# The last scatter of a streaming MoE step: identity products that add x in PSUM, multiplies that read PSUM, sample stores on ScalarE, and a 1 MB transfer in two rows

## Chip, core and metric

The kernel runs on one core of one Trainium2 chip. The metric is device time in microseconds. Engines are named as in the profile: PE is TensorE (PEld its weight loads), DVE is VectorE, ACT is ScalarE, POOL is GpSimd, SP is SyncE; a q behind a name is the engine's own instruction queue, which also issues DMAs.

## The reference

One layer of an encoder trunk for 256 prompt tokens and 32 sample tokens of width 1024, all in float32: a modulated RMS norm, an input projection, a pooling mixer and a convolution module, gates and an output projection, and then a mixture of experts and a final norm. The change touches only what follows the last expert:

```python
x = x + g1 * (merged @ w_out)
h2 = _rms_norm(x, norm2_g) * (1.0 + sc2) + sh2
# 32 experts of 1024 x 1024, top 4 by a router:
#   gt = min(t @ Wg + bg, 7);  up = clip(t @ Wu + bu, -7, 7)
#   out += combine[:, e] * ((gt * sigmoid(1.702 gt) * (up + 1)) @ Wd + bd)
x = x + g2 * _moe(h2, ...)
y = x * rsqrt(mean(x * x) + 1e-6) * final_g        # prompt and sample
```

## The kernel before

Tokens lie on partitions: `x[:, 0]` and `x[:, 1]` hold 128 prompt tokens each, and the 32 sample tokens are spread as `xs`, four quarters of 256 features on four groups of 32 partitions.

The experts run as items, an item being up to 64 tokens of one expert; here there are 33 for 32 experts. In an item PE multiplies the gathered tokens by the expert's gate, up and down matrices (`product`, whose inner matmul is L1731: 16 matmuls of 512 columns for one matrix, each of which has two rows in the trace). DVE evaluates the down product into `ysb`, scaled by the gate g2 (L1306). PE then puts the item's rows back at their tokens by products with the weighted one-hot matrix `ohwT` (L1758 for the prompt, L1749 for the sample). It does so inside the next item, and DVE adds the result to `x` (L1269, L1265). A product of the scatter has only 64 rows to sum over: half hh of the features lies on partitions 64 hh to 64 hh + 63, so two products, one for each half, use different halves of the PE array and different PSUM banks.

The last item has no next one, so its scatter stands alone behind the loop. PE waits for `y_ev` (the first half of `ysb`, all of it for the sample) and makes the products for prompt tile 0, the sample and tile 1 (L1845, L1749). DVE adds each to `x` (`last_add`, L1316; the sample at L1336), ACT squares the sums and accumulates them (`last_squares`, L851; L856), DVE takes the mean (`last_mean`, L1319), ACT the root (`last_root`, L846), and DVE the reciprocal and the product with `final_g` (`finish`, L1328, L1330). The sample's sum of squares has four parts on four groups of partitions; a product on PE adds these up (L1849). SP stores the outputs in the order in which they are made: tile 0 (L539), the sample in four pieces (L537), tile 1 in two halves (L544).

Weights stream from HBM on SP's queue through 18 slots of SBUF, a pair of slots (2 MB) at a time. PE raises `piece_used` when a piece may be overwritten, and SP waits for it before each load. `LAST_HALVES` names the pairs of the last expert that come in two transfers of 1 MB each, so that `product` can start on the first half (L513). The very last is the second half of the last down pair; PE waits for it before k = 6, the seventh of the eight steps over the contraction. The order of all instructions is written out by hand, for each engine.

## Time and profile before

| | us |
|---|---|
| time, median of 3 runs (lowest, highest) | 1152.16 (1151.28, 1153.07) |
| profiled execution: span from first to last instruction | 1150.3 |
| PE busy | 1122.8 (98%) |
| DVE busy | 497.9 (43%) |
| ACT busy | 181.4 (16%) |
| HBM read | 454.40 MB, 396 GB/s over the span |
| span behind the last expert product (1137.7 to 1150.3) | 12.6 |

The trace gives the span of the profiled execution; the time of a run holds what lies around such a span too. The median of the timed runs is 1.86 us above the span. Busy time says how long an engine had an instruction in work; matmul rows overlap, since one starts before the last results of the one before have come out.

### The profile page before, as it was taken

The numbers are of one execution on the slowest core, as the hardware profiler recorded it, in microseconds if no ns is written. First come the engines' busy times: TensorE is split into PE (matmuls) and PEld (weight loads), VectorE is DVE, ScalarE is ACT, GpSimd is POOL, SyncE is SP. The second block draws the span as 40 slices with busy tenths as digits, with TensorE's granted clock in tenths as the row PEclk, the third lists the DMA queues.
The fourth block names the chain that finished last, engine by engine and source line by source line (L and its number), as shares of the span: only waits on it lengthen the run. The fifth ranks groups of instructions, "written<-read, shape, count | busy, mean of one in ns | idle before, by whom it ended". The sixth has DMA issues, their size and how long they took to land.

```text
span 1150.3 us, 16135 instructions
## 1 busy us (share of the span) xinstructions
PE 1122.8 (98%) x5962; PEld 457.5 (40%) x5963; DVE 497.9 (43%) x1134; ACT 181.4 (16%) x343; POOL 29.8 (3%) x78
## 2 busy tenths in 40 slices
PE   8999999999999999999999999999999999999996
PEld 6676675633333333333333333333333333333332
DVE  3498425653344433444333433343334433333334
ACT  4101301311111111111111111111111111111112
POOL 4002300000000000000000000000000000000000
PEclk9999999999999999999999999999999999999999
DMA  9988688699999999999999999999999999999995
GB/s 342 374 288 297 245 305 303 229 419 417 427 428 428 428 428 428 428 428 428 428 428 428 428 428 428 428 428 428 428 428 428 428 428 428 428 428 429 426 422 228
DMA packets 59022, 456.15 MB, mean 397 GB/s; under 512 B 7237, under 2 KB 26497, under 8 KB 31349
## 3 DMA queue, kind: packets, MB, share of 16 engines
q1 hardware_dynamic: 54880, 452.35, 94.9%
q10 hardware_dynamic: 4117, 3.47, 1.2%
q8 instruction: 16, 0.26, 0.1%
q14 instruction: 9, 0.07, 0.0%
HBM read 454.40 MB, written 1.40 MB: 396 GB/s over the span
## 4 chain that ended last, share of the span: by engine, by line
PE 77%; DMA 21%; DVE 1%; issue 0%; SPq 0%; ACT 0%; DVEq 0%
PE bank L1731 46%; DMA arena<-in_exp_w_up 10%; DMA arena<-in_exp_w_gate 10%; PE bank L1509 6%; PE bank L1456 4%; PE bank L1758 4%; PE bank L1675 4%; PE bank L1596 2%; PE bank L1813 1%; PE bank L1579 1%; PE bank L1683 1%; PE bank L1430 1%; PE bank L1749 1%; PE bank L1687 1%; PE bank L1378 1%; PE bank L1689 0%
## 5 line engine op out<-in xcount | busy, mean ns | idle before, releaser
L1731 PE MATMUL bank<-ring,arena 128*64 128x512 f32 x2112 | 469.9, 595 | 10.2 <-DMA ring<-in_exp_w_gate 9.7
L1731 PEld LDWEIGHTS bank<-ring,arena 128*64 128x64 f32 x2112 | 146.3, 137 | 310.0 <-issue 283.7
L1731 PE MATMUL bank<-arena 128*64 128x512 f32 x1056 | 235.9, 595 | 4.2 <-DMA arena<-in_exp_w_gate 4.0
L1731 PEld LDWEIGHTS bank<-arena 128*64 128x64 f32 x1056 | 73.6, 137 | 153.8 <-issue 138.5
L821 ACT ACTIVATE arena<-arena 32x256 f32<-32x256 f32 x136 | 56.0, 412 | 421.1 <-DVE arena L1200 419.9
L1291 DVE TENSOR_SCALAR arena<-bank 128x512 f32<-128x512 f32 x33 | 22.8, 691 | 166.6 <-PE bank L1731 166.6
L1284 DVE TENSOR_SCALAR arena<-bank 128x512 f32<-128x512 f32 x33 | 22.8, 691 | 166.5 <-PE bank L1731 166.5
L1306 DVE TENSOR_TENSOR arena<-bank,biases 128x512 f32<-128x512 f32 x66 | 42.5, 686 | 109.9 <-PE bank L1731 109.9
L1269 DVE TENSOR_TENSOR x<-x,bank 128x512 f32<-128x512 f32 x132 | 84.5, 681 | 12.6 <-PE bank L1758 12.6
L834 ACT ACTIVATE arena<-arena 128x512 f32<-128x512 f32 x33 | 20.8, 629 | 353.8 <-DVE arena L1284 353.8
L1758 PE MATMUL bank<-arena 64*128 64x512 f32 x264 | 65.6, 615 | 0.0
L1509 PE MATMUL bank<-arena,ring 128*128 128x288 f32 x256 | 64.4, 409 | 0.0
L1675 PE MATMUL bank<-h,arena 128*64 128x512 f32 x268 | 63.3, 592 | 0.0
L969 DVE SCALAR_TENSOR_TENSOR h<-h,arena 128x318 f32<-128x318 f32 x120 | 55.5, 541 | 0.0
L1509 PEld LDWEIGHTS bank<-arena,ring 128*128 128x128 f32 x256 | 48.1, 190 | 17.1 <-issue 4.2
L1456 PE MATMUL bank<-arena,ring 128*128 128x288 f32 x192 | 47.7, 408 | 0.5 <-DVE arena L922 0.5
L834 ACT ACT_TABLE_LOAD x33 | 42.3, 1283 | 0.6
L1456 PEld LDWEIGHTS bank<-arena,ring 128*128 128x128 f32 x192 | 36.2, 190 | 12.0 <-issue 1.7
L1687 PE MATMUL bank<-biases,mine 32*64 32x288 f32 x264 | 40.0, 414 | 0.0
L1758 PEld LDWEIGHTS bank<-arena 64*128 64x128 f32 x264 | 22.7, 186 | 42.3 <-issue 42.3
L1205 DVE COPY arena<-arena 32x256 f32<-32x256 f32 x136 | 38.4, 282 | 2.5
L1683 PE MATMUL bank<-biases,mine 32*64 32x512 f32 x136 | 37.4, 613 | 0.0
(312 smaller groups left out, 739.8 us busy)
## 6 DMA issues: line engine op xcount, KB each, us to landing
ring<-in_exp_w_gate SPq DMA_DIRECT2D x42, 2048.0 KB, 27.8
ring<-in_exp_w_up SPq DMA_DIRECT2D x41, 2048.0 KB, 28.2
ring<-in_exp_w_down SPq DMA_DIRECT2D x40, 2048.0 KB, 29.1
arena<-in_exp_w_gate SPq DMA_DIRECT2D x21, 2048.0 KB, 25.7
arena<-in_exp_w_up SPq DMA_DIRECT2D x20, 2048.0 KB, 27.3
arena<-in_exp_w_down SPq DMA_DIRECT2D x20, 2048.0 KB, 30.0
ring<-in_w_ada SPq DMA_DIRECT2D x24, 1024.0 KB, 10.7
ring<-in_gate_w SPq DMA_DIRECT2D x8, 1024.0 KB, 8.6
```

The source lines that it names most:

```text
L821: ins = a.activation(*square_moves(1, s, u), ACT.Copy)
L834: a.activation(gsig, gmin, ACT.Sigmoid, scale=ALPHA).then_inc(gsig_ready, 1)
L969: ins = v.scalar_tensor_tensor(out=yc[:, c, :], in0=uc_ext[:, c, k:k + CW], scalar=tap, in1=yc[:, c, :], op0=ALU.mult, op1=ALU.add)
L1269: ins = v.tensor_tensor(x[:, t, cs], x[:, t, cs], scatter_bank(t, hh), ALU.add)
L1306: v.tensor_tensor(ysb[:, gg, :], bank[5][:, :], g2h[:, gg, :], ALU.mult).then_inc(y_ev, 1)
L1456: ins = mm(bank[n % 4][:, 0:TOK], w[:, k, P * (n % 2):P * (n % 2 + 1)], (hS if n < UNSHIFTED else hT)[:, k, :], start=(k == 0), stop=(n >= ...
L1509: ins = mm(bank[n % 4][:, 0:TOK], w[:, k, P * (n % 2):P * (n % 2 + 1)], hT[:, k, :], start=(k == 0), stop=(k == KD - 1))
L1675: ins = mm(bank[0][64 * hh:64 * hh + 64, :], oh[:, t, :], half_rows(h2[:, t, :], hh), start=start, stop=stop, skip_group_check=True)
L1683: mm(bank[3][out, :], mine[B_GATE, :], bias_rows[B_GATE, cs], start=True, stop=False, skip_group_check=True)
L1687: found = mm(bank[6 + i][out, 0:TOK], mine[LOOKUP, :], routedT[:, i, :], start=True, stop=True, skip_group_check=True)
L1731: ins = mm(out[64 * hh:64 * hh + 64, :], lhs(k), w[:, D * (k % 2) + HALF * hh:D * (k % 2) + HALF * (hh + 1)], start=(done is y_mm and k == ...
L1758: ins = mm(scatter_bank(t, hh), ohwT[64 * hh:64 * hh + 64, P * t:P * (t + 1)], ysb[64 * hh:64 * hh + 64, 0, :], start=True, stop=True, ski ...
```

## The change

It does five things, four of them behind the last item.

- Identity products add `x` in PSUM. `carry` multiplies the identity by `x`, which starts the sum in the bank, and the scatter product adds to it there. Tile 0's two banks and the sample's are filled ahead of the wait for `y_ev`; tile 1's two banks are filled one by one between scatter products. The sample's sum is in bank 1 in place of bank 5.
- The four additions on DVE for the prompt and the one for the sample are gone. ACT squares what is in PSUM, DVE's final multiplies read PSUM, and tile 0 is multiplied in two halves rather than in one instruction.
- The mean of a tile is no longer an addition and a scaling on DVE: DVE scales the first half's sum, and ACT's root takes the second half's sum as input with the first as its bias. The two memsets of accumulators move ahead of the item loop.
- ACT issues the sample's four stores, behind its last root. SP issues tile 0 and tile 1's halves.
- The last transfer of 1 MB, 128 partitions of 8 KB, becomes two of 4 KB per partition. PE waits for the first before k = 6 and for the second (`last_ld`) before k = 7.

```diff
-            def refill_halves(e, q, before):
+            def refill_halves(e, q, before, rows_apart=False):
 ...
+                    if half and rows_apart:
+                        for r, landed in enumerate((pair_ld[p], last_ld)):
+                            at_row = SLOT * half + D * r
+                            sp.dma_start(slots(2 * p + half, 1)[:, D * r:D * (r + 1)], w[:, i % 2, at_row:at_row + D]).then_inc(landed, 16)
+                        continue
 ...
+                refill_halves(last_turn, at_last + i, (at_last + i - PAIRS) // PER_EXPERT, rows_apart=(i == LAST_HALVES[-1]))
 ...
-            for i, t in enumerate((0, 2, 1)):
-                sp.wait_ge(y_ready, i + 1)
-                if t == 2:
-                    for q in range(4):
-                        sp.dma_start(quarter(y_sample[0], q), y_s[32 * q:32 * q + 32, :]).then_inc(stored, 16)
-                elif t == 0:
-                    sp.dma_start(y_prompt[0, 0:P, :], ybuf[:, 0, :]).then_inc(stored, 16)
-                else:
-                    for hh in range(2):
-                        sp.wait_ge(y_ready, i + 1 + hh)
-                        cs = slice(HALF * hh, HALF * (hh + 1))
-                        sp.dma_start(y_prompt[0, P:2 * P, cs], ybuf[:, 1, cs]).then_inc(stored, 16)
+            sp.wait_ge(y_ready, 2)
+            sp.dma_start(y_prompt[0, 0:P, :], ybuf[:, 0, :]).then_inc(stored, 16)
+            for hh in range(2):
+                sp.wait_ge(y_ready, 4 + hh)
+                cs = slice(HALF * hh, HALF * (hh + 1))
+                sp.dma_start(y_prompt[0, P:2 * P, cs], ybuf[:, 1, cs]).then_inc(stored, 16)
 ...
-            def last_root(t, nth):
+            def last_root(t, nth, scale=1.0, rest=None):
                 act.wait_ge(mean2, 3 + nth)
-                a.activation(stat[:, 4 + t:5 + t], stat[:, 8 + t:9 + t], ACT.Sqrt).then_inc(sqrt_ready, 1)
-
-            def last_squares(t):
-                for hh in range(2):
-                    act.wait_ge(x3_ready, 3 * t + hh + 1)
-                    a.activation(ring[:, JUNK + t, HALF * hh:HALF * (hh + 1)], x[:, t, HALF * hh:HALF * (hh + 1)],
-                                 ACT.Square, accum_out=stat[:, 18 + 3 * hh + t:19 + 3 * hh + t]).then_inc(ssq3, 1)
-
-            last_squares(0)
-            act.wait_ge(x3_ready, 3)
-            a.activation(ring[:, JUNK + 2, 0:D // 4], xs, ACT.Square, accum_out=part_sum[:, 0:1]).then_inc(parts_ready, 1)
-            last_root(0, 1)
-            last_squares(1)
+                a.activation(stat[:, 4 + t:5 + t], rest if rest is not None else stat[:, 8 + t:9 + t], ACT.Sqrt, scale=scale,
+                             bias=stat[:, 8 + t:9 + t] if rest is not None else 0.0).then_inc(sqrt_ready, 1)
+
+            def last_squares(t, hh):
+                act.wait_ge(last_mm, 3 * t + hh + 1)
+                a.activation(ring[:, JUNK + t, HALF * hh:HALF * (hh + 1)], last_bank(t, hh),
+                             ACT.Square, accum_out=stat[:, 18 + 3 * hh + t:19 + 3 * hh + t]).then_inc(ssq3, 1)
+
+            last_squares(0, 0)
+            last_squares(0, 1)
+            act.wait_ge(last_mm, 3)
+            a.activation(ring[:, JUNK + 2, 0:D // 4], last_sample, ACT.Square, accum_out=part_sum[:, 0:1]).then_inc(parts_ready, 1)
+            act.wait_ge(ssq3, 2)
+            last_root(0, 1, 1.0 / D, stat[:, 21:22])
+            last_squares(1, 0)
+            last_squares(1, 1)
             last_root(2, 2)
-            last_root(1, 3)
+            act.wait_ge(ssq3, 4)
+            last_root(1, 3, 1.0 / D, stat[:, 22:23])
+            act.wait_ge(y_ready, 3)
+            for q in range(4):
+                act.dma_start(quarter(y_sample[0], q), y_s[32 * q:32 * q + 32, :]).then_inc(stored, 16)
 ...
+            v.memset(part_sum, 0.0)
+            v.memset(stat[:, 18:24], 0.0)
 ...
-            dve.wait_ge(ssq2, 6)
             dve.wait_ge(y_ev, items * 2 + 2)
             dve.sem_inc(last_y, 1)
-            v.memset(part_sum[:, :], 0.0)
-            v.memset(stat[:, 18:24], 0.0)
-            def last_add(t, hh):
-                cs = slice(HALF * hh, HALF * (hh + 1))
-                dve.wait_ge(last_mm, 3 * t + hh + 1)
-                v.tensor_tensor(x[:, t, cs], x[:, t, cs], last_bank(t, hh), ALU.add).then_inc(x3_ready, 1)
 
             def last_mean(t, total):
                 v.tensor_scalar(stat[:, 8 + t:9 + t], total, 1.0 / D, EPS, ALU.mult, ALU.add).then_inc(mean2, 1)
 
-            def tile_mean(t):
-                dve.wait_ge(ssq3, 2 * t + 2)
-                step(v.tensor_tensor(stat[:, t:t + 1], stat[:, 18 + t:19 + t], stat[:, 21 + t:22 + t], ALU.add))
-                last_mean(t, stat[:, t:t + 1])
-
-            def finish(t, nth, parts):
+            def last_gain(t, nth):
                 dve.wait_ge(sqrt_ready, 4 + nth)
                 step(v.reciprocal(stat[:, 4 + t:5 + t], stat[:, 4 + t:5 + t]))
-                for out, src, gain in parts:
-                    v.scalar_tensor_tensor(out=out, in0=src, scalar=stat[:, 4 + t:5 + t], in1=gain,
-                                           op0=ALU.mult, op1=ALU.mult).then_inc(y_ready, 1)
-
-            last_add(0, 0)
-            last_add(0, 1)
-            dve.wait_ge(last_mm, 3)
-            v.tensor_tensor(xs, xs, bank[5][:, 0:D // 4], ALU.add).then_inc(x3_ready, 1)
-            last_add(1, 0)
-            tile_mean(0)
-            last_add(1, 1)
+
+            def finish(t, out, src, gain):
+                v.scalar_tensor_tensor(out=out, in0=src, scalar=stat[:, 4 + t:5 + t], in1=gain,
+                                       op0=ALU.mult, op1=ALU.mult).then_inc(y_ready, 1)
+
+            halves = [slice(HALF * hh, HALF * (hh + 1)) for hh in range(2)]
+            dve.wait_ge(ssq3, 1)
+            last_mean(0, stat[:, 18:19])
+            dve.wait_ge(fg_ld, 16 * 5)
+            last_gain(0, 1)
+            finish(0, ybuf[:, 0, halves[0]], last_bank(0, 0), fgb[:, halves[0]])
             dve.wait_ge(parts_mm, 1)
             last_mean(2, bank[2][:, 0:1])
-            dve.wait_ge(fg_ld, 16 * 5)
-            finish(0, 1, [(ybuf[:, 0, :], x[:, 0, :], fgb)])
-            tile_mean(1)
-            finish(2, 2, [(y_s, xs, fgq)])
-            halves = [slice(HALF * hh, HALF * (hh + 1)) for hh in range(2)]
-            finish(1, 3, [(ybuf[:, 1, cs], x[:, 1, cs], fgb[:, cs]) for cs in halves])
+            dve.wait_ge(ssq3, 3)
+            last_mean(1, stat[:, 19:20])
+            finish(0, ybuf[:, 0, halves[1]], last_bank(0, 1), fgb[:, halves[1]])
+            last_gain(2, 2)
+            finish(2, y_s, last_sample, fgq)
+            last_gain(1, 3)
+            for hh, cs in enumerate(halves):
+                finish(1, ybuf[:, 1, cs], last_bank(1, hh), fgb[:, cs])
 ...
+                    elif last and done is y_mm and k == KD - 1:
+                        pe.wait_ge(last_ld, 16)
 ...
-            def scatter_sample():
+            def scatter_sample(out=bank[5][:, 0:D // 4], start=True):
 
                 for half in range(2):
                     for hh in range(2):
                         q = 2 * hh + half
-                        ins = mm(bank[5][32 * q:32 * q + 32, 0:D // 4], ohwT[64 * hh:64 * hh + 64, 2 * P:TOK],
-                                 ysb[64 * hh:64 * hh + 64, 1, D // 4 * half:D // 4 * (half + 1)], start=True, stop=True,
+                        ins = mm(out[32 * q:32 * q + 32, :], ohwT[64 * hh:64 * hh + 64, 2 * P:TOK],
+                                 ysb[64 * hh:64 * hh + 64, 1, D // 4 * half:D // 4 * (half + 1)], start=start, stop=True,
                                  skip_group_check=True)
 ...
-            pe.wait_ge(y_ev, items * 2 + 1)
             pe.wait_ge(ohwT_ev, items + 1)
             pe.wait_ge(scat_add, items * 2 + 1)
             pe.wait_ge(up_read, items + 1)
-            for t in (0, 2, 1):
-                if t == 2:
-                    pe.wait_ge(last_y, 1)
-                    scatter_sample().then_inc(last_mm, 1)
-                    continue
-                for hh in range(2):
-                    mm(last_bank(t, hh), ohwT[64 * hh:64 * hh + 64, P * t:P * (t + 1)], ysb[64 * hh:64 * hh + 64, 0, :],
-                       start=True, stop=True, skip_group_check=True).then_inc(last_mm, 1)
+
+            def carry(out, src):
+                mm(out, ident[:, :], src, start=True, stop=False, skip_group_check=True)
+
+            def last_scatter(t, hh):
+                mm(last_bank(t, hh), ohwT[64 * hh:64 * hh + 64, P * t:P * (t + 1)], ysb[64 * hh:64 * hh + 64, 0, :],
+                   start=False, stop=True, skip_group_check=True).then_inc(last_mm, 1)
+
+            for hh in range(2):
+                carry(last_bank(0, hh), x[:, 0, HALF * hh:HALF * (hh + 1)])
+            carry(last_sample, xs)
+            pe.wait_ge(y_ev, items * 2 + 1)
+            for hh in range(2):
+                last_scatter(0, hh)
+            carry(last_bank(1, 0), x[:, 1, 0:HALF])
+            pe.wait_ge(last_y, 1)
+            scatter_sample(last_sample, start=False).then_inc(last_mm, 1)
+            last_scatter(1, 0)
+            carry(last_bank(1, 1), x[:, 1, HALF:D])
+            last_scatter(1, 1)
```

PE behind the last expert product. L1845 are the scatter products of a prompt tile, L1749 (L1751 after) those of the sample, L1842 the identity products, and the last row the sum of the sample's parts. Before:

```order
L1845 MATMUL bank6<-arena 128x512 [waits up_read,scat_add,ohwT_ev]
L1845 MATMUL bank7<-arena 128x512
L1749 MATMUL bank5<-arena 32x256 [waits last_y]
L1749 MATMUL bank5<-arena 32x256 x3
L1845 MATMUL bank3<-arena 128x512
L1845 MATMUL bank4<-arena 128x512
L1849 MATMUL bank2<-arena 128x4 [waits parts_ready,same_made]
```

After:

```order
L1842 MATMUL bank6<-x,ident 128x512 [waits up_read,scat_add]
L1842 MATMUL bank7<-x,ident 128x512
L1842 MATMUL bank1<-arena,ident 128x256
L1845 MATMUL bank6<-arena 128x512 [waits y_ev]
L1845 MATMUL bank7<-arena 128x512
L1842 MATMUL bank3<-x,ident 128x512
L1751 MATMUL bank1<-arena 32x256 [waits last_y]
L1751 MATMUL bank1<-arena 32x256 x3
L1845 MATMUL bank3<-arena 128x512
L1842 MATMUL bank4<-x,ident 128x512
L1845 MATMUL bank4<-arena 128x512
L1862 MATMUL bank2<-arena 128x4 [waits parts_ready,same_made]
```

Three identity products now stand ahead of the scatter of tile 0 (banks 6 and 7), and one stands ahead of each scatter product of tile 1 (banks 3 and 4), so that these two no longer follow each other. The wait for `y_ev` has moved behind the first three.

DVE at the same place, from the first addition to the first final multiply (L1330, 1024 columns) and the mean behind it. L1319 is `last_mean`; L1323 adds two halves' sums. Before:

```order
L1316 TENSOR_TENSOR x<-x,bank6 128x512 [waits last_mm]
L1316 TENSOR_TENSOR x<-x,bank7 128x512 [waits last_mm]
L1336 TENSOR_TENSOR arena<-arena,bank5 128x256 [waits last_mm]
L1316 TENSOR_TENSOR x<-x,bank3 128x512 [waits last_mm]
L1323 TENSOR_TENSOR stat<-stat 128x1 [waits ssq3]
L1319 TENSOR_SCALAR stat<-stat 128x1 [waits chain_v]
L1316 TENSOR_TENSOR x<-x,bank4 128x512 [waits last_mm]
L1319 TENSOR_SCALAR stat<-bank2 128x1 [waits parts_mm]
L1328 RECIPROCAL stat<-stat 128x1 [waits sqrt_ready,fg_ld]
L1330 SCALAR_TENSOR_TENSOR h2<-x,stat,ring 128x1024 [waits chain_v]
L1323 TENSOR_TENSOR stat<-stat 128x1 [waits ssq3]
L1319 TENSOR_SCALAR stat<-stat 128x1 [waits chain_v]
```

After, from the first mean (L1322) to the last final multiply (L1329):

```order
L1322 TENSOR_SCALAR stat<-stat 128x1 [waits y_ev,ssq3]
L1326 RECIPROCAL stat<-stat 128x1 [waits sqrt_ready,fg_ld]
L1329 SCALAR_TENSOR_TENSOR h2<-bank6,stat,ring 128x512 [waits chain_v]
L1322 TENSOR_SCALAR stat<-bank2 128x1 [waits parts_mm]
L1322 TENSOR_SCALAR stat<-stat 128x1 [waits ssq3]
L1329 SCALAR_TENSOR_TENSOR h2<-bank7,stat,ring 128x512
L1326 RECIPROCAL stat<-stat 128x1 [waits sqrt_ready]
L1329 SCALAR_TENSOR_TENSOR h2<-bank1,stat,ring 128x256 [waits chain_v]
L1326 RECIPROCAL stat<-stat 128x1 [waits sqrt_ready]
L1329 SCALAR_TENSOR_TENSOR h2<-bank3,stat,ring 128x512 [waits chain_v]
L1329 SCALAR_TENSOR_TENSOR h2<-bank4,stat,ring 128x512
```

The additions are gone, and so are the ones of sums. The wait for `parts_mm`, the last product on PE, stood ahead of all final multiplies; now it stands behind the first of them and ahead of the other four.

## Rows read from the trace of the kernel before

**Rows 1.** Busy time by stage: us, then each engine's busy us, clock, DMA, GB/s
```profile
1110.35:1137.70 27.35, 27.34 (x144) 9.46 (x144) 10.21 (x23) 4.17 (x8) 0.00 (x0) 1.00 0.90 368
1137.70:1150.30 12.60, 3.11 (x18) 1.08 (x18) 8.20 (x21) 3.46 (x13) 0.00 (x0) 0.83 0.26 94
```

**Rows 2.** TensorE's last expert product, timeline: start us, us, engine, line
```profile
1130.61 7.09 PE L1731 MATMUL bank<-ring,arena 128*64 128x512 f32 x32
```

**Rows 3.** TensorE's weight loads around the last transfer's landing, timeline
```profile
1135.42 0.14 PEld L1731 LDWEIGHTS bank<-ring,arena 128*64 128x64 f32 x2 [0.32 <-DMA ring<-in_exp_w_down]
1135.81 0.14 PEld L1731 LDWEIGHTS bank<-ring,arena 128*64 128x64 f32 x2 [0.25 <-issue]
```

**Rows 4.** SyncE's DMA issues: last weight transfers and the three kinds of store
```profile
1098.01 10.93 SPq L513 DMA_DIRECT2D ring<-in_exp_w_down  x2
...
1144.49 0.37 SPq L539 DMA_DIRECT2D out<-h  x1
1145.34 1.73 SPq L537 DMA_DIRECT2D out<-h  x4
1147.17 0.84 SPq L544 DMA_DIRECT2D out<-h  x2
```

**Rows 5.** All engines from the last expert product's end, timeline
```profile
1137.75 1.29 DVE L1306 TENSOR_TENSOR arena<-bank,biases 128x512 f32<-128x512 f32 x2 [3.33 <-PE bank L1731]
...
1138.68 1.13 PE L1845 MATMUL bank<-arena 64*128 64x512 f32 x4 [0.98 <-DVE arena L1306]
...
1139.74 0.64 PE L1749 MATMUL bank<-arena 64*32 64x256 f32 x8
...
1139.81 1.28 DVE L1316 TENSOR_TENSOR x<-x,bank 128x512 f32<-128x512 f32 x2 [0.49 <-PE bank L1845]
...
1140.31 1.13 PE L1845 MATMUL bank<-arena 64*128 64x512 f32 x4
...
1140.53 0.63 ACT L851 ACTIVATE ring<-x 128x512 f32<-128x512 f32 x1 [5.27 <-DVE x L1316]
...
1142.41 0.36 PE L1849 MATMUL bank<-arena 128*128 128x4 f32 x2 [0.98 <-ACT ring L856]
...
1142.92 0.15 DVE L1319 TENSOR_SCALAR stat<-bank 128x1 f32<-128x1 f32 x1
...
1143.17 0.61 ACT L851 ACTIVATE ring<-x 128x512 f32<-128x512 f32 x1
...
1143.78 0.19 ACT L846 ACTIVATE stat<-stat 128x1 f32<-128x1 f32 x1
...
1144.83 0.48 DVE L1330 SCALAR_TENSOR_TENSOR h<-arena,stat,ring 128x256 f32<-128x256 f32 x1
...
1145.42 1.41 DVE L1330 SCALAR_TENSOR_TENSOR h<-x,stat,ring 128x512 f32<-128x512 f32 x2
```

**Rows 6.** TensorE where one expert follows another with no stall, timeline
```profile
302.82 7.09 PE L1731 MATMUL bank<-arena 128*64 128x512 f32 x32
309.74 1.46 PE L1731 MATMUL bank<-ring,arena 128*64 128x512 f32 x6
```

**Rows 7.** TensorE: products over 128 rows, then scatter products over 64 rows
```profile
184.90 7.13 PE L1596 MATMUL bank<-ring,arena 128*128 128x512 f32 x16
...
1117.37 1.99 PE L1758 MATMUL bank<-arena 64*128 64x512 f32 x8
```

**Rows 8.** A ScalarE read of PSUM, by line and form: busy us, mean ns
```profile
L673 ACT ACTIVATE arena<-bank 128x512 f32<-128x512 f32 x1 | 0.6, 597 | 0.6 <-PE bank L1378 0.6
```

**Rows 9.** What SyncE waited for at the end, and ScalarE's slowest DMA issues
```profile
SPq L90 <- DMA out<-h: 1.9, 1, 1.9
...
L732 ACTq DMA_DIRECT2D out<-biases x16: 875/885/1015, 133.6 to 150.9; - x16
```

**Rows 10.** Landing times of 1 MB and 512 KB transfers, first 230 us, by tile
```profile
ring<-in_exp_w_down SPq DMA_DIRECT2D x2, 1024.0 KB, 5.4
...
ring<-in_pool_w SPq DMA_DIRECT2D x1, 512.0 KB, 3.7
```

4 lines of the change are left out of this document (2 added, 2 removed).

## The prediction

> **What bounds the kernel now.** I read first the busy time by stage. From 1110.35 us PE is busy for 27.34 of 27.35 us, so the last expert runs at PE's pace. Behind it lie 12.6 us in which PE is busy for 3.11, DVE for 8.20 and ACT for 3.46 [rows 1]: a chain of short steps, each waiting for the one before. All but one edit of the change lie in these 12.6 us, and that one, the split transfer, ends just ahead of them.
>
> Then the timeline of that chain [rows 5]. The last expert product starts at 1130.61 [rows 2], and DVE takes up its result at 1137.75. PE starts the scatter at 1138.68 and has it done 1.13 later for tile 0 and at 1141.44 for tile 1. DVE adds from 1139.81, ACT squares from 1140.53 to 1143.78, and DVE's multiplies end at 1146.83 (1145.42 + 1.41).
>
> Last, SP's queue [rows 4]. Tile 0 is stored at 1144.49. The sample's four issues take 1145.34 to 1147.07. Tile 1's first half is ready at about 1146.13 (half of the 1.41), but is issued at 1147.17, and the second half, ready at 1146.83, at about 1147.59. So the queue of stores, and not DVE, sets the last 0.75 us. SP then waits 1.9 for the data [rows 9].
>
> **The change, part by part.**
>
> Transfer in two rows. The last product's 16 matmuls take 0.43 each (6.92 / 16 [rows 6]), a step k has two of them, so k = 6 starts 12 x 0.43 behind 1130.61, at 1135.8, and its weights are loaded one matmul ahead. That load was released by the DMA at 1135.42 and the next stands at 1135.81 [rows 3]: the megabyte came some 0.04 late at most, and the product still took the 7.09 us of one that waits for nothing [rows 2, 6]. I cost the gain at 0. In a run where the megabyte is later, the split can take away one step k, 0.86, at most. SP issued the megabyte some 25 us ahead (1098.01 + 10.93 [rows 4]), so one more issue costs it nothing. The loss is a rival below.
>
> Identity products on PE. Eight products over 128 rows of 512 columns took 7.13 us [rows 7]. In a stream a row outlasts the next one's start by 0.17 (7.09 against 6.92 [rows 6]), so one costs (7.13 - 0.17) / 8 = 0.87, and the one of 256 columns 0.44. The same rows show also that PE passes from one expert to the next, registers and branch included, with no gap, so the first three start at 1130.61 + 6.92 = 1137.53 and end at 1139.71. They hide the wait for `y_ev`, which let PE start at 1138.68 [rows 5], but are longer than it by 1.03. Tile 0's pair of scatter products then takes 1.13 to its end [rows 5], 1140.84. ACT squares from there, and no longer from 1140.53: the addition of about 0.7 that is gone is more than eaten.
>
> Tile 1 is worse off. Two pairs of scatter products took 1.99 [rows 7], some 0.95 for a pair, that is, two products over 64 rows ran in little more than the time of one full product. The change parts tile 1's pair. No row shows such a product alone. From below it is half a pair, 0.48; from above a whole pair, 0.95; I take the 0.87 of a full product, because the columns to stream are the same and a pair costs hardly more. Then: identity from 1140.66, sample 1141.53, and 0.57 later (1139.74 to 1140.31 [rows 5]) the scatter at 1142.10, identity 1142.97, scatter 1143.84. PE is free at 1144.71, where before tile 1 was done by 1141.44: 3.3 later.
>
> ACT and DVE behind it. ACT's last square starts at about 1144.9 and its roots follow 0.61 later [rows 5], done by 1145.8. DVE's chain is longer. The sum of the sample's parts starts at 1144.71, and DVE reads it 0.51 later (1142.41 to 1142.92 [rows 5]), at 1145.22. Until then the second multiply of tile 0 is queued behind that wait, with DVE idle from about 1143.8. Then come two means, 0.25 (0.15 each by the row, partly overlapped, an estimate); tile 0's second half, 0.69 (half of 1.28 or 1.41 [rows 5]); a reciprocal, 0.11; the sample and its reciprocal, 0.59 (1144.83 to 1145.42 [rows 5]); and tile 1's halves, 1.41. The last output is ready at 1148.27, against 1146.83 before: 1.44 later.
>
> ACT reading PSUM instead of SBUF: 0.597 for a copy of 512 columns [rows 8] against 0.61 to 0.63 for the squares [rows 5]: nothing. DVE reading PSUM: additions from PSUM took 0.64 each, multiplies from SBUF 0.70 [rows 5]: nothing to pay either. The Trainium skill, VectorE: DVE Perf Modes, in its errata section, gives VectorE a fixed part of 58 cycles for SBUF sources and 120 for PSUM, at 0.96 GHz: 0.065 us more for each read of PSUM, an estimate from that page. By it the four multiplies that end the chain would cost 0.26 more and the sum would be 1153.0. The rows do not bear it out.
>
> The memsets ahead of the loop are two of DVE's shortest instructions, and PE has the whole first gate product to cover them: 0.
>
> Stores. SP has tile 0 at 1146.2, tile 1's first half at 1147.57 and its second at 1148.3; before these were issued at 1144.49, 1147.17 and 1147.59. The last issue is 0.7 later, the last but one 0.4. When the second half is issued, the first is still on its way, so the end follows something between: I take 0.55. Moving the sample's issues to ACT thus gives back 0.75 us or so of the 1.44 lost. On ACT they start at 1146.9 and, at SP's 0.43 each [rows 4], are done at 1148.6, level with SP's.
>
> Sum: identity products and unpaired scatter +1.44, the queue of stores -0.75 to -1.05, the rest 0: +0.4 to +0.7, say +0.55. The profiled execution would have a span of 1150.85 in place of 1150.3. The timed median lies 1.86 above the span, so 1152.16 + 0.55 = 1152.7 us. What this measurement can tell from no change is 0.2%, 2.3 us, and the forecast is a quarter of that.
>
> **Rivals.**
>
> Better overlap. If an unpaired product costs 0.48, PE is free 0.78 earlier and all behind it too: 1151.9. If in the timed runs the last megabyte is later than in the trace, the split takes up to 0.86 away: 1151.1. Against it: the product with no stall in the trace. For a gain of over 2.3 us I find no row: all that is removed on the chain is five additions and the queue of stores.
>
> Stores on ACT. This one ends slower. ACT's own issues of small stores took 0.875 to 1.015 each [rows 9], where SP's took 0.43. With four at 1.015 from 1146.9 the last is issued at 1150.96, the data take up to 1.9, and the close 0.4 as before: span 1153.3, which is 3.0 more, 1155.2. It decides from about 0.83 each. Against it: those had many short pieces of 512 bytes, and the sample's have 32 of 1 KB.
>
> The second row late. Alone, a 1 MB transfer of expert weights landed in 5.4 and one of 512 KB in 3.7 [rows 10]. Two of 3.7 one behind the other would be 2.0 longer: the last row at 1137.4 rather than 1135.4, needed for the load of k = 7 at 1136.3, so PE stops for 1.1: 1153.8. Against it: both rows are issued long before their turn in a queue that is full, so they follow each other without a gap. The rule that 1 MB is the size from which the bandwidth is near its best (the Trainium skill, DMA: Bandwidth & Descriptors, section Bandwidth) would speak for this rival, and a fixed part of 2.0 us for each transfer, which the same page gives, would cost about as much. Only the landing in the changed trace can tell.
>
> That the change doesn't do what it says is no rival I can give a time: that SP's sample stores go and the additions go stands in the order.
>
> **How the numbers follow.** Forecast 0.68 (1152.7, own range 1151.9 to 1153.6); better overlap 0.17 (1151.1 to 1151.9); stores on ACT 0.08 (1153.6 to 1155.2); second row late 0.07 (1153.8). The runs before spread by 0.9 to either side of the median, which I add to the ends. For 8 in 10, I leave out the far ends of the rivals: 1151.2 to 1154.4. Faster by over 2.3 us needs something that I do not see, 0.04; slower by as much (above 1154.5) is the upper half of the ACT rival, and the others with the runs' spread of 0.9 on top, 0.09; within it 0.87.
>
> **What would show it.** In the changed trace: three identity products from 1137.5, counted from a last expert product at the same place; tile 0's scatter a microsecond later than before; tile 1's last scatter ending 3 us later; DVE idle ahead of the mean of the sample; the last multiply ending 1.4 later, and tile 1's stores issued as soon as it is ready. Wrong would be: a gap in the last down product before k = 7, ACT's issues outlasting SP's, unpaired products at half the time, or any shift ahead of 1110 us, since nothing there should move.

## The result, and the profile after

The changed kernel took 1156.63 us (median of 6 runs, 1155.12 to 1162.28), the kernel before 1151.91 beside it (6 runs, 1151.28 to 1153.07): ratio 1.0040, 95% interval 1.0023 to 1.0058. Measured again with 12 and 36 runs it was 1.0019 [1.0010, 1.0029], +2.2 us (1.2 to 3.3). So it is slower, by 1.2 us at the least and some 2 by the second, tighter measurement, where +0.55 (1152.7) was forecast. The profiled execution took 1155.12, its span is 1153.4, against 1150.3 before: 3.1 more.

All that the change touches, but the split transfer and the two early memsets, lies behind the last expert product. I cut the span in two ways: at that product's end for the busy times, and at its start for the lengths that are compared below. Busy time by stage (stretch, length, then PE, PEld, DVE, ACT and POOL, granted clock, DMA share, GB/s); the first two rows answer to [rows 1], the third is the part of the second in which PE is never idle:

```profile
1111.16:1138.51 27.35, 27.35 (x145) 9.54 (x145) 10.29 (x23) 4.17 (x8) 0.00 (x0) 1.00 0.91 374
1138.51:1153.40 14.89, 8.50 (x28) 2.92 (x28) 5.27 (x13) 3.66 (x13) 0.00 (x0) 0.83 0.22 80
1138.51:1147.01 8.50, 8.50 (x28) 2.92 (x28) 2.36 (x5) 2.93 (x10) 0.00 (x0) 1.00 0.00 1
```

The last stage is 14.89 long instead of 12.6. PE is busy for 8.50 of it instead of 3.11, DVE for 5.27 instead of 8.20: the work went from an engine that had time in the gaps to one that now runs 8.50 us without one, at a clock of 1.00. The other part of the 3.1 lies ahead: the last product starts 0.81 later than in [rows 2]. From its start to the end of the span ("the tail", below) it is 1153.4 - 1131.42 = 21.98 us, before 1150.3 - 1130.61 = 19.69: **+2.29**. Spans are given to 0.1 us, so a tail is good to 0.05 and the difference of two tails to 0.1.

TensorE in the tail, timeline of the changed kernel (start us, busy us; the rows of the weight loads, PEld, say in brackets how long the loader had been idle):

```profile
1131.42 7.09 PE L1733 MATMUL bank<-ring,arena 128*64 128x512 f32 x32
...
1138.43 1.98 PE L1842 MATMUL bank<-x,ident 128*128 128x512 f32 x4
...
1140.26 0.59 PE L1842 MATMUL bank<-arena,ident 128*128 128x256 f32 x2
...
1140.78 1.13 PE L1845 MATMUL bank<-arena 64*128 64x512 f32 x4
1141.84 0.30 PEld L1842 LDWEIGHTS bank<-x,ident 128*128 128x128 f32 x2 [0.76 <-issue]
1141.84 1.12 PE L1842 MATMUL bank<-x,ident 128*128 128x512 f32 x2
...
1142.90 0.64 PE L1751 MATMUL bank<-arena 64*32 64x256 f32 x8
...
1143.46 1.12 PE L1845 MATMUL bank<-arena 64*128 64x512 f32 x2
...
1144.51 1.13 PE L1842 MATMUL bank<-x,ident 128*128 128x512 f32 x2
...
1145.57 1.12 PE L1845 MATMUL bank<-arena 64*128 64x512 f32 x2
1146.62 0.30 PEld L1862 LDWEIGHTS bank<-arena 128*128 128x128 f32 x2 [0.76 <-issue]
1146.62 0.39 PE L1862 MATMUL bank<-arena 128*128 128x4 f32 x2
```

The product of 32 matmuls takes 7.09, as it did with the megabyte whole. Read the starts. A full product in the middle of a stream of its own shape (rows x columns of weights) takes 0.86 from its start to the next: two matmuls of 0.43. The first one behind another shape takes 0.11 more, since its two matmuls start 0.54 apart (1138.43 and 1138.97), and the last one ahead of another shape 0.09 more. So each change of shape costs 0.2. From 1140.78 on, every product stands between two other shapes, and the next start comes 1.05 to 1.06 later: 1141.84, then 1142.90, then 1143.46 to 1144.51, 1145.57, 1146.62. The loader's rows show what is different. At such a place the next weights are loaded only when the next product starts (1141.84 and 1141.84), not ahead of it. From tile 0's pair to the sum of parts there are six changes of shape; with 0.86 for a product or a pair and 0.2 for a change that is 5 x 0.86 + 0.36 for the sample (0.56 - 0.2) + 6 x 0.2 = 5.86, where the rows have 1146.62 - 1140.78 = 5.84. From the first identity product to the sum of parts it is 8.19 us; the prediction had 7.18.

DVE and ACT behind it:

```profile
1141.94 0.60 ACT L852 ACTIVATE ring<-bank 128x512 f32<-128x512 f32 x1 [5.87 <-PE bank L1845]
...
1144.60 0.75 DVE L1329 SCALAR_TENSOR_TENSOR h<-bank,stat,ring 128x512 f32<-128x512 f32 x1
...
1146.73 0.60 ACT L852 ACTIVATE ring<-bank 128x512 f32<-128x512 f32 x1 [1.42 <-PE bank L1845]
1147.05 0.16 DVE L1322 TENSOR_SCALAR stat<-bank 128x1 f32<-128x1 f32 x1 [1.70 <-PE bank L1862]
...
1147.18 0.74 DVE L1329 SCALAR_TENSOR_TENSOR h<-bank,stat,ring 128x512 f32<-128x512 f32 x1
...
1148.62 1.41 DVE L1329 SCALAR_TENSOR_TENSOR h<-bank,stat,ring 128x512 f32<-128x512 f32 x2
```

DVE waits 1.70 for PE's sum, with the second multiply of tile 0 queued behind that wait, and ends at 1150.03: 18.61 behind the product's start, before 16.22 (1145.42 + 1.41 - 1130.61). Of the +2.29, +2.39 is there by the last multiply. The stores give back 0.10.

The stores: the issues in the timeline, then what SyncE waited for at the end, then one line of ScalarE's issues (min/median/max in ns) and their landing (us):

```profile
1147.95 0.37 SPq L541 DMA_DIRECT2D out<-h  x1
...
1148.55 2.00 ACTq L868 DMA_DIRECT2D out<-h  x4
...
1149.40 0.99 SPq L545 DMA_DIRECT2D out<-h  x2
```

```profile
SPq L90 <- DMA out<-h: 2.6, 1, 2.6
```

```profile
L868 ACTq DMA_DIRECT2D out<-h x4: 353/446/656, 1148.5 to 1150.1; - x4
...
DMA to landing us min/median/max: 2.2/2.4/2.9
```

SP issues tile 1's second half as soon as it is there, and then waits 2.6 where it had waited 1.9 [rows 9]. ACT's four issues fill 2.00 us. The last starts at 1150.1 and the slowest lands in 2.9: 1153.0. The sample's last store, and not tile 1's, is then the last to land.

The 0.81 ahead of the tail is not in the code that the change edits. In the changed kernel's profiled execution TensorE's granted clock stood at 0.50 (the 1.2 GHz level) from 22 to 25 us, with PE busy throughout. In the 8 us ahead PE had been busy for 7.25, as in that of before. The pooled mixing (L1368) starts at 31.46:

```profile
22.00:24.00 2.00, 2.00 (x5) 1.43 (x6) 1.92 (x10) 1.19 (x4) 0.00 (x0) 0.50 1.11 311
```

```profile
31.46 1.05 PE L1368 MATMUL bank<-arena 4*32 4x512 f32 x4
```

In before the clock was 1.00 (2.4 GHz) there and the row stands at 29.83:

```profile
22.00:24.00 2.00, 2.00 (x9) 1.58 (x10) 1.93 (x10) 1.20 (x4) 0.00 (x0) 1.00 1.12 317
```

```profile
29.83 1.05 PE L1368 MATMUL bank<-arena 4*32 4x512 f32 x4
```

1.63 us are lost by there, and 0.81 of them are left at the last product. The difference is found again in PE's idle time ahead of the expert products, 9.4 us in all, 8.9 of it by the transfers (page of after, busy us, mean ns, idle before):

```profile
L1733 PE MATMUL bank<-ring,arena 128*64 128x512 f32 x2112 | 469.9, 595 | 9.4 <-DMA ring<-in_exp_w_gate 8.9
```

The same row of before has 10.2 and 9.7: PE came later to transfers that set the pace there, and waited less.

### The profile page after: what moved, and what is told of

It is laid out like the page before. It is cut to its first block, busy times and chain, and to the rows that moved or that the text cites. A ratio compares the mean times of both kernels' runs of the same rounds, so it can differ in the third digit from the quotient of the medians.

```text
span 1153.4 us, 16151 instructions
## 1 busy us (share of the span) xinstructions
PE 1129.3 (98%) x5972; PEld 460.1 (40%) x5973; DVE 498.1 (43%) x1128; ACT 181.4 (16%) x343; POOL 29.7 (3%) x78
## 4 chain that ended last, share of the span: by engine, by line
PE 78%; DMA 21%; DVE 1%; issue 0%; SPq 0%; ACT 0%; DVEq 0%
PE bank L1733 45%; DMA arena<-in_exp_w_up 10%; DMA arena<-in_exp_w_gate 10%; PE bank L1509 5%; PE bank L1456 4%; PE bank L1760 4%; PE bank L1675 4%; PE bank L1596 2%; PE bank L1815 1%; PE bank L1579 1%; PE bank L1683 1%; PE bank L1430 1%; PE bank L1751 1%; PE bank L1687 1%; PE bank L1378 1%; PE bank L1689 0%
## 5 line engine op out<-in xcount | busy, mean ns | idle before, releaser
L1279 DVE TENSOR_TENSOR x<-x,bank 128x512 f32<-128x512 f32 x132 | 84.6, 682 | 12.6 <-PE bank L1760 12.6
L1689 PE MATMUL bank<-h,arena 32*64 32x512 f32 x136 | 37.4, 613 | 0.0
```

Source lines behind the costliest of these rows:

```text
L1279: ins = v.tensor_tensor(x[:, t, cs], x[:, t, cs], scatter_bank(t, hh), ALU.add)
```

## The experiments

**Theory T:** the tail's 2.3 us come from PE: products of another shape one behind the other cost 1.06 instead of 0.87, so all behind the sum of parts is later, and the stores on ACT add a little at the end. **Rival R1:** the split transfer costs it. **R2:** the stores on ACT cost it. **R3:** VectorE's queue, or its reads of PSUM. The table has what was measured; each run is then told with what was expected. Ratios are those to the kernel before on the same chip, of 11 or 12 runs each (the first of after is of 6), against 17 to 36 of the kernel before; "tail" and "last multiply" come from one profiled execution each and are counted from the start of the last expert product.

| run | ratio [95%] | tail | last multiply ends | SP's last wait |
|---|---|---|---|---|
| before | | 19.69 | 16.22 | 1.9 |
| after | 1.0040 [1.0023, 1.0058] | 21.98 | 18.61 | 2.6 |
| e1 after again | 1.0019 [1.0010, 1.0029] | 22.05 | 18.61 | 2.7 |
| e2 megabyte whole | 1.0021 [1.0010, 1.0031] | 22.03 | 18.61 | 2.6 |
| e3 before + split | 1.0005 [0.9994, 1.0015] | 19.75 | 16.22 | 1.9 |
| e4 before + ACT stores | 0.9996 [0.9986, 1.0006] | 19.32 | 16.22 | 2.3 |
| e5 tile 0 in halves | 1.0010 [0.9993, 1.0028] | 21.61 | 18.61 | 2.2 |
| e6 grouped products | 1.0006 [0.9993, 1.0020] | 20.97 | 17.70 | 2.5 |
| e7 DVE order | 1.0009 [0.9995, 1.0023] | 21.27 | 18.32 | 2.2 |
| e8 after, SP stores | 1.0032 [1.0014, 1.0049] | 22.34 | 18.61 | 1.9 |
| e9 sample's identity only | 0.9997 [0.9980, 1.0014] | 19.29 | 16.26 | 2.2 |
| e10 tile 1 added | 1.0011 [1.0002, 1.0020] | 20.44 | 17.40 | 2.2 |
| e11 no identity | 1.0016 [0.9992, 1.0040] | 19.90 | 16.96 | 2.2 |
| e12 e9, mean earlier | 0.9995 [0.9986, 1.0003] | 18.59 | 15.66 | 2.2 |

**e1: the changed kernel once more**, without an edit.

> The changed kernel once more, for a second trace and a second time. The two traces so far differ by 3.1 us in span, of which 0.8 lies ahead of the last expert. My theory: these 0.8 come from the 3.4 us at the lower clock at 22 to 25 us of that one execution and are no part of the change; then a trace without that dip has the last product start near 1130.6, and the median is the tail's 2.3 us above the kernel before (1154.2). The rival, something ahead of the tail that the change makes slower: the last product starts at 1132 or later although the clock is 1.0 throughout, and the time is again 4 to 5 above the kernel before.

Tail 22.05 and 1.0019, +2.2 us: the tail repeats within 0.07, and this time it is the whole of the difference. The clock is 1.00 at 22 us, and the last product starts at 1130.45, as the theory wanted. The first measurement's +4.7 did not come back: the changed kernel's median was 1.6 lower than there (1155.05) and that of the kernel before 1.2 higher (1153.07).

**e2: the changed kernel, last megabyte in one transfer.**

```
-  refill_halves(last_turn, ..., rows_apart=(i == LAST_HALVES[-1]))
+  refill_halves(last_turn, ...)
-      elif last and done is y_mm and k == KD - 1:
-          pe.wait_ge(last_ld, 16)
```

> The changed kernel with the last megabyte in one transfer again. If the split row by row costs nothing, as I forecast, it has the time of the changed kernel within 0.5 us. If the split is where the time goes that the tail doesn't explain (a later landing, or loads of the last expert that drain more slowly), it is 1.5 to 2.5 faster.

**e3: the kernel before with the split alone** (the second row counted on another semaphore that is free by then).

```
+  if half and rows_apart:
+      for r, landed in enumerate((pair_ld[p], c_ld)):
+          sp.dma_start(... row r ...).then_inc(landed, 16)
 ...
+      elif last and done is y_mm and k == KD - 1:
+          pe.wait_ge(c_ld, 48)
```

> The kernel before with only the last megabyte split. By my theory within 0.5 us of the kernel before; by the rival 1.5 to 2.5 slower. The second row is counted on a semaphore of the first loads, because there is none to spare.

```profile
1130.95 7.09 PE L1738 MATMUL bank<-ring,arena 128*64 128x512 f32 x32
```

Again 7.09, and the tail moves by 0.02 (e2 against e1) and 0.06 (e3 against before). By time e3 is 1.0005, and e2's 1.0021 stands beside e1's 1.0019; its median is 0.65 above e1's, a little outside the 0.5 that I allowed, but the intervals cover each other. R1 falls from both sides: the split neither costs nor gives. In a run whose megabyte came late it might still give; none of the fourteen traces has one.

**e4: the kernel before with the sample's stores on ACT.**

```
 # SP: the four sample stores go
+act.wait_ge(y_ready, 2)
+for q in range(4):
+    act.dma_start(quarter(y_sample[0], q), y_s[32 * q:32 * q + 32, :]).then_inc(stored, 16)
```

> The kernel before with only the sample's four stores issued by ScalarE. By my sum SP can issue tile 1's halves at 1146.2 and 1146.9 in place of 1147.2 and 1147.6, so it is 0.5 to 0.75 faster (1151.3). By the rival, stores from two queues finish each other later (2.6 us of waiting at the end of the changed kernel against 1.9 before), and the gain is 0 to 0.2.

```profile
1145.66 0.37 SPq L538 DMA_DIRECT2D out<-h  x1
...
1146.51 2.07 ACTq L862 DMA_DIRECT2D out<-h  x4
...
1147.41 0.95 SPq L543 DMA_DIRECT2D out<-h  x2
```

The tail is 0.37 shorter, between the 0.5 to 0.75 of my sum and the 0 to 0.2 of the rival: R2 falls, the stores on ACT are a gain, but half of what the queue had cost (0.75). SP's last wait grew from 1.9 to 2.3. This is shown by the tail alone; the times (0.9996) leave it open.

**e5: tile 0 stored in two halves**, so that its first half leaves early.

```
-sp.wait_ge(y_ready, 2)
-sp.dma_start(y_prompt[0, 0:P, :], ybuf[:, 0, :]).then_inc(stored, 16)
+for hh in range(2):
+    sp.wait_ge(y_ready, 1 + hh)
+    sp.dma_start(y_prompt[0, 0:P, cs], ybuf[:, 0, cs]).then_inc(stored, 16)
```

> The changed kernel with tile 0 stored in two halves as soon as each is multiplied. The changed kernel waits 2.6 us for its stores, the one before 1.9. Theory S: 1.19 MB of stores now leave within 2.5 us and the wait is for bandwidth; then 256 KB leave 1.7 us earlier, the wait falls to 2.1 or less, and the tail from the last expert product's start (22.0 us) gets 0.4 to 0.6 shorter. Rival: the wait is longer because stores of two queues (SP and ACT) mix; then the halves change nothing.

Tail 21.61, 0.37 less than after's, all of it behind the last multiply, which still ends 18.61 behind the product. ACT's issues took 1.79 instead of 2.00, and landed in 1.6 to 2.3 instead of 2.2 to 2.9. So the store of the whole of tile 0, issued 0.6 ahead of the sample's, had stood in their way. The gain is just short of the forecast (0.4 to 0.6, with a wait of 2.1 or less: it was 2.2). It is not that store alone: in e8, where it is as close, the sample's stores land in 1.6 to 2.3 as well, but there SP issues them and tile 1's halves wait behind. What slows them in the changed kernel is a store ahead and stores of the other queue beside them; how much each is was not parted further.

**e6: the same products, grouped by shape**: from tile 0's pair to the sum of parts four changes of shape instead of six, and tile 1's pair kept.

```
-carry(last_bank(1, 0), x[:, 1, 0:HALF])
+for hh in range(2):
+    carry(last_bank(1, hh), x[:, 1, HALF * hh:HALF * (hh + 1)])
 scatter_sample(...)
-last_scatter(1, 0)
-carry(last_bank(1, 1), x[:, 1, HALF:D])
-last_scatter(1, 1)
+for hh in range(2):
+    last_scatter(1, hh)
```

> The changed kernel with tile 1's two identity products one behind the other, then the sample, then tile 1's two scatter products as a pair. Theory P: a product costs 0.86 when the next has its shape and 1.06 when it doesn't (the next weights are loaded late), and two scatter products of different halves run together. Then PE is done 1.06 + 0.2 = 1.25 us earlier (the last product starts 6.95 behind the first identity product in place of 8.19), and the tail is 1.0 to 1.3 shorter. Rival: scatter onto a started sum is slow by itself (1.06 each, pair or not); then PE gains 0.2 only.

```profile
1137.85 1.98 PE L1842 MATMUL bank<-x,ident 128*128 128x512 f32 x4
...
1140.19 1.13 PE L1845 MATMUL bank<-arena 64*128 64x512 f32 x4
...
1141.25 1.98 PE L1842 MATMUL bank<-x,ident 128*128 128x512 f32 x4
...
1143.16 0.64 PE L1751 MATMUL bank<-arena 64*32 64x256 f32 x8
1143.73 1.13 PE L1845 MATMUL bank<-arena 64*128 64x512 f32 x4
...
1144.79 0.38 PE L1862 MATMUL bank<-arena 128*128 128x4 f32 x2
```

The same eleven products take 6.94 from the first identity product to the sum, as T had said (6.95), against 8.19. The two identity products of tile 1 take 1.91 (0.96 and 0.95, 0.2 above two of 0.86), and the two scatter products of tile 1 1.06 together, where they had been 1.05 each, so the rival falls. Of the 1.25, two changes fewer are 0.4 and the pair that is kept 0.86. Tail -1.01. That is the test of T: an order of PE's products, with nothing else changed, is worth a microsecond. The time (1.0006) does not stand apart from e1's by its interval; the trace does.

**e7: VectorE's second multiply of tile 0 ahead of its wait for the sum.**

```
 finish(0, ybuf[:, 0, halves[0]], last_bank(0, 0), fgb[:, halves[0]])
+finish(0, ybuf[:, 0, halves[1]], last_bank(0, 1), fgb[:, halves[1]])
 dve.wait_ge(parts_mm, 1)
 ...
-finish(0, ybuf[:, 0, halves[1]], last_bank(0, 1), fgb[:, halves[1]])
```

> The changed kernel with tile 0's second multiply ahead of the wait for the sample's sum of parts, on VectorE. In the changed trace VectorE is idle for 1.70 us there with that multiply behind it. If that order is on the chain, its 0.70 goes off it and tile 0 is stored 1.8 us earlier: the tail is 0.7 to 1.2 shorter. Rival: ScalarE's roots bound what follows; then the tail gains at most 0.2 from the sample on.

```profile
1142.91 1.41 DVE L1329 SCALAR_TENSOR_TENSOR h<-bank,stat,ring 128x512 f32<-128x512 f32 x2
...
1144.35 0.37 SPq L541 DMA_DIRECT2D out<-h  x1
...
1145.36 0.16 DVE L1322 TENSOR_SCALAR stat<-bank 128x1 f32<-128x1 f32 x1 [1.04 <-PE bank L1862]
...
1145.86 0.16 DVE L1326 RECIPROCAL stat<-stat 128x1 f32<-128x1 f32 x1 [0.28 <-ACT stat L847]
```

The last multiply ends only 0.29 earlier although 0.74 of work left the chain, because DVE then waits 0.28 for ACT's roots, which that multiply had covered. ACT's last square is bound by PE too. The tail is 0.71 shorter. The rest lies in the stores: tile 0 is now stored 2.2 us ahead of the sample (1144.35 against 1146.57), and ACT's stores land in 1.5 to 2.4, as in e5. R3's queue is real, but second to PE.

**e8: the changed kernel, sample's stores back on SP.**

```
 # SP, between tile 0 and tile 1
+sp.wait_ge(y_ready, 3)
+for q in range(4):
+    sp.dma_start(quarter(y_sample[0], q), y_s[32 * q:32 * q + 32, :]).then_inc(stored, 16)
 # ACT: the same four go
```

> The changed kernel with the sample's stores issued by SP again, between tile 0's and tile 1's. By the queue's arithmetic: four issues of 0.43 from 1148.5 hold tile 1's first half until 1150.25 and its second until 1150.7, where ACT's issue let them go at 1149.4 and 1150.1, so the tail is 0.6 longer. By the rival of mixed queues: the shorter wait at the end gives most of that back, 0 to 0.2 longer.

```profile
1149.28 1.99 SPq L544 DMA_DIRECT2D out<-h  x4
...
1151.32 0.90 SPq L548 DMA_DIRECT2D out<-h  x2
```

Tail 22.34, 0.36 longer than after's, between the queue's arithmetic and the rival; in e4 the same move was worth 0.37. SP's four issues cost 1.99 here, before 1.73 [rows 4].

**e9: only the sample gets an identity product.** The tiles' scatter products run in pairs, tile 1 ahead of the sample, and VectorE adds them to x as before. Kept from the change: ACT's stores, the sample read from PSUM, the early memsets. Tile 0 is stored in halves, the megabyte is whole.

```
+carry(last_sample, xs)
 pe.wait_ge(y_ev, items * 2 + 1)
+pair(0); pair(1)
 pe.wait_ge(last_y, 1)
+scatter_sample(last_sample, start=False).then_inc(last_mm, 1)
 # DVE: four additions to x, the sample's goes
```

> The kernel before with an identity product for the sample only (0.43, inside PE's wait for y_ev), both prompt tiles' scatter pairs one behind the other and then the sample, additions on VectorE as before, the root that takes the second half's sum, tile 0 stored in halves and the sample stored by ScalarE. Tail means the time from the last expert product's start to the span's end: 19.7 in the kernel before, 22.0 in the changed one. If VectorE's work is what bounds the kernel before there, 0.41 of addition and some 0.3 of small steps go, and with the stores the tail is 18.5 to 19.0. Rival: ScalarE's row of squares bounds it instead (five squares and three roots, 3.5 us, from 1140.5); then it is 19.2 to 19.5.

```profile
1136.62 0.70 PE L1846 MATMUL bank<-arena,ident 128*128 128x256 f32 x2
...
1137.49 1.99 PE L1850 MATMUL bank<-arena 64*128 64x512 f32 x8 [0.16 <-DVE arena L1313]
...
1141.04 0.15 DVE L1326 TENSOR_SCALAR stat<-stat 128x1 f32<-128x1 f32 x1
...
1141.62 0.29 ACT L841 ACTIVATE stat<-stat 128x1 f32<-128x1 f32 x1 [0.56 <-DVE stat L1326]
```

Without the tiles' identity products the tail is 19.29: 2.69 less than after's (0.37 of it by the halves of tile 0), 0.40 less than before's. Against before the gain is one of the stores, as in e4: the last multiply ends at 16.26, before at 16.22. I had expected 18.5 to 19.0, and the rows show why it was missed: VectorE's mean of tile 0 stands behind four additions, and ACT waits 0.56 for it with two squares queued.

**e10: identity products for tile 0 and the sample, tile 1 added by VectorE.**

```
+for hh in range(2):
+    carry(last_bank(0, hh), x[:, 0, HALF * hh:HALF * (hh + 1)])
 carry(last_sample, xs)
 pe.wait_ge(y_ev, items * 2 + 1)
+pair(0, start=False); pair(1)
```

> The kernel e9_sample_identity with identity products for tile 0 as well, which VectorE and ScalarE then read in PSUM; tile 1 still added on VectorE. It asks what tile 1's identity products alone cost in the changed kernel. By the account that PE is the bound there (8.19 us from the first identity product to the sum of parts), PE is now free 3 us sooner and the tail falls from 22.0 to 19.8 to 20.2, still above e9, because the two identity products of tile 0 start the chain 0.9 later and VectorE fills up behind. Rival: products onto started sums are as cheap as others and the changed kernel's loss is in VectorE's order; then it stays above 21.

Tail 20.44, a little more than expected: 1.15 above e9's for tile 0's identity products. They outlast the wait that was to hide them: the scatter starts 9.37 behind the expert product (1139.93 - 1130.56), in e9 7.88 (1137.49 - 1129.61). What is left to after's 21.98 is 1.54, of which the store of tile 0 in halves explains 0.37 (e5): tile 1's identity products and parted pair cost some 1.2.

**e11: no identity product at all**, otherwise e9 (the sample's addition is back on VectorE).

> The kernel e9_sample_identity with no identity product at all: the sample is added on VectorE, between the tiles. If the sample's identity product is worth its addition, the tail is 0.3 to 0.5 longer than that of e9. If it is worth nothing because ScalarE is the bound, the two are equal within 0.1.

Tail 19.90, 0.61 more than e9's, somewhat above the 0.3 to 0.5 of the forecast. The sample's product, which fits into PE's wait for `y_ev` (0.16 of that wait is left in e9, and the scatter starts no later for it: 7.88 behind the expert product, here 7.97), is the one identity product that pays. That holds for the order of e9 and e11, which is worse by itself than before's: with no identity product in either, the last multiply ends at 16.96 here and at 16.22 before. Whether the product pays in before's own order was not run.

**e12: e9 with VectorE's first mean between the third and the fourth addition.**

```
 for t in range(2):
     for hh in range(2):
+        if t and hh:
+            dve.wait_ge(ssq3, 1)
+            last_mean(0, stat[:, 18:19])
         last_add(t, hh, 2 * t + hh + 1)
```

> e9 with VectorE's first mean (stat of tile 0) moved from behind its four additions to between the third and the fourth. In the trace of e9 ScalarE waited 0.56 us for that mean. Theory: ScalarE's root of tile 0, its two squares of tile 1 and the multiplies behind them come 0.4 to 0.6 earlier; from the start of the last expert product to the end of the span 18.7 to 18.9, against 19.29 in e9, 19.69 before and 21.98 in the changed kernel, first-order time 0.8 to 1.0 below before (ratio about 0.9992), which the timing can hardly tell from none. Rival: the roots are not on the chain that ends last (tile 1's square, the sample or the store of the last half is), then 19.2 to 19.3 as in e9.

```profile
1132.81 7.09 PE L1738 MATMUL bank<-ring,arena 128*64 128x512 f32 x32
...
1143.65 0.14 DVE L1326 TENSOR_SCALAR stat<-stat 128x1 f32<-128x1 f32 x1
...
1144.22 0.29 ACT L841 ACTIVATE stat<-stat 128x1 f32<-128x1 f32 x1
...
1147.05 1.42 DVE L1333 SCALAR_TENSOR_TENSOR h<-x,stat,ring 128x512 f32<-128x512 f32 x2
```

ACT's wait is gone, and the tail is 18.59, 0.70 less than e9's and 1.10 less than before's; a little more than expected. It has the shortest tail of all kernels here. By time it is 0.9995 [0.9986, 1.0003]: that it beats the kernel before is shown by the tail alone; the times leave it open.

## Why the prediction was wrong

**Split transfer, cost 0: right.** 7.09 in every trace; e2 and e3.

**First three identity products, 1137.53 to 1139.71: right in kind.** They start 7.01 behind the expert product (predicted 6.92) and take 2.35 (2.18): +0.26 for both. The cost is the one of the next step: 0.09 where the shape changes ahead of them, and 0.2 for the rest of that change and the one behind them. I had both at nothing.

**"Unpaired product 0.87, pair 0.95": the step that failed.** The mechanism (tile 1's pair parted, all behind the sum of parts later) was right, the size was not. Four unpaired products took 1.06, 1.05, 1.06 and 1.05, and the pair 1.06: +0.85. With the +0.26 that is the 1.1 by which the sum of parts comes later than I had it: 3.3 later than tile 1 was done before had become 4.4. I had taken 0.87 from a stream of eight products of one shape [rows 7], and bounded it by half a pair and a whole pair, so the true value lay outside my bounds. The lower came from half a pair, the upper from two pairs of one shape, where 0.2 for the change is shared by two. The rows that would have told stood in [rows 5]: tile 0's pair starts at 1138.68 and the sample, of another shape, at 1139.74, 1.06 later and not 0.95. The Trainium skill speaks of this, and I had not weighed it: TensorEngine Tiling (Array Packing), section Key Properties, says that a change of tiling mode drains TensorE. It names no price. The trace agrees in kind: 1.06 in place of 0.86, 0.2 us for each change, and e6 gave back 1.25 us by grouping (two changes fewer, and a pair kept). That the engine drains is the Trainium skill's word; the rows show late weight loads and later starts.

**DVE behind the sum, 3.56 to the last multiply: right** (3.41). DVE's and ACT's reads of PSUM cost what I had them at, about nothing: a square 0.60 and a multiply 0.74 to 0.75 alone, two of them 1.41 as from SBUF. The 0.065 more for each read that I had estimated from the Trainium skill (VectorE: DVE Perf Modes, errata section) is not seen: e12's multiply from SBUF takes 1.42 for two, e7's from PSUM 1.41. In both the second operand comes from SBUF.

**"The queue of stores gives back 0.75 to 1.05": failed too, by 0.65 to 0.95.** From the last multiply to the end of the span it was 3.47 before (1150.3 - 1146.83) and 3.37 after: 0.10. Moving the four issues is worth 0.36 (e8) or 0.37 (e4), not 0.75, because ACT's last issue starts as late as SP's last and lands later (up to 2.9). The rest goes to tile 0's store, which the new order of the multiplies brings close to the sample's: 0.37 in e5. My rival "stores on ACT" had asked for 0.83 an issue; it was 0.45 in the median, 0.50 with the gaps. But the 0.83 does not follow from my own sum: ACT's last issue, three issues behind 1146.9, passes SP's at 1148.3 from 0.47 each. With 0.50 it stands at 1150.10 in the changed trace, SP's at 1150.05, and it lands 0.5 later (2.9 against 2.4). The landing, which I had left at 1.9, does the rest.

Together: +0.09 and +1.01 on PE, -0.15 on DVE, +0.79 at the stores, is +1.74, and 20.24 predicted (1150.85 - 1130.61) becomes 21.98. So the forecast of +0.55 for the tail was +2.3, and e1 measures +2.2 by time.

**The rest of the first measurement is open.** +4.7 at first, +2.2 in e1; their intervals overlap between 1.0023 and 1.0029. The profiled executions show where time can lie that is not in the tail: the first expert product starts anywhere from 228.5 to 230.7, in kernels of either kind (before 228.88, after 230.51, e1 228.62, e9 228.71, e12 230.28), and part of it is left at the last product (before 1130.61, after 1131.42, e12 1132.81). The traces part into two groups. In eight of the fourteen the pooled mixing starts at 31.1 us or later (in the other six at 30.3 or earlier), and in each of them PE was slow for a while ahead of it. In after, e6, e8 and e11 it is the low clock at 22 us (0.50 to 0.61 granted). In e3, e4, e5 and e12 no such row stands there, but the same products from 6 us on take up to 1.8 times as long as in before, although the profile gives the clock as 1.00 there. Before, then e3:

```profile
6.07 1.05 PE L1368 MATMUL bank<-arena 4*32 4x512 f32 x4
7.05 2.94 PE L1357 MATMUL bank<-ones,ident 128*128 128x128 f32 x24
```

```profile
6.08 1.92 PE L1373 MATMUL bank<-arena 4*32 4x512 f32 x4
7.92 4.57 PE L1362 MATMUL bank<-ones,ident 128*128 128x128 f32 x24
```

I had written that no shift ahead of 1110 us should occur; one did. It comes in kernels that have only one part of the change (e3 the split, e4 ACT's stores) and in e11, which has no identity product, so it does not need these products. Whether the change makes such fronts likelier (what it edits runs 900 us and more behind them, but the early memsets and the code of every engine are other than before) was not tried, and one trace of each kernel can't tell. The first six runs held more than such a front: the profiled one had the late front and was the shortest of them (1155.12).

## What to carry to other kernels

Before work is moved to the engine that is ahead, ask whether it fits into that engine's own wait: the sample's identity product did (0.6 gained, e11 against e9), the four of the tiles did not, although each replaced an addition of 0.64 to 0.69. As the change placed them, 2.3 were lost (e9 against after without the 0.37 of e5); that holds the parted pair and the changes of shape too. Grouped as in e6 they would still lose some 1.3 by the same sum (20.97 - 0.37 - 19.29). Price a product from a row in which its neighbour has another shape, and group products by shape. A tail of 20 us is best compared from a fixed event, here the last expert product's start: it repeated within 0.1 us, where times needed 12 runs for an interval of 0.1%.

## What the runs showed of the hardware

- fp32 products on TensorE at a granted clock of 1.00: 0.86 from start to start for 128 x 128 weights and 512 columns within a stream of one shape, 1.05 to 1.06 for one between two other shapes, 1.91 for two (e6). So a change of shape costs 0.2, 0.11 of it behind the change and 0.09 ahead of it. Two products of 64 rows side by side take 1.06 between other shapes, two such pairs 1.91 (e9: 1137.49 to 1139.40), and one of 64 rows alone 1.05. So parting a pair costs a whole product.
- Stores of 32 KB from SBUF to HBM landed 2.2 to 2.9 us after their issue from ACT beside SP's (after), 1.9 to 2.5 in e4, and 1.5 to 2.4 where half or all of the 512 KB ahead of them had left some 2 us earlier or more (e5, e7). From SP they landed in 1.6 to 2.3 (e8). ACT's issues took 0.35 to 0.72 each (after, e4); SP's four 1.73 to 1.99.
- Four of fourteen executions had a granted clock of 0.50 to 0.61 (the 1.2 GHz level for most of the stretch) in the 2 us from 22 us, with PE busy for 1.95 to 2.00 of them; after stood 1.63 us later than before at 31 us.
